# A state-space scan taken two steps at a time, its lagged matrices formed beside the attention, and pieces of the modulation moved

## The reference

```python
def s5_mixer(h, ...):
    u32 = (h @ w_in).reshape(B, L, N_GROUPS, GROUP_CH)     # 64 groups of 16 channels
    dt = jnp.exp(log_dt)[:, None]
    mag = jnp.exp(lr * dt)                                 # decay, per group and state (64 states)
    ab_re, ab_im = mag * jnp.cos(li * dt), mag * jnp.sin(li * dt)
    ...                                                    # bb: b scaled by coef_re, coef_im
    bu_re = jnp.einsum('blgc,gpc->blgp', u32, bb_re)       # bu_im likewise
    x[l] = ab * x[l-1] + bu[l]                             # complex, over the 256 steps
    y = einsum('blgp,gcp->blgc', xr, c_re) - einsum('blgp,gcp->blgc', xi, c_im)
    y = y + d_skip * u32
    g = jax.nn.gelu(y)
    return (g * jax.nn.sigmoid(g @ w_glu + b_glu)) @ w_out

def modulation(cs, w, b):                                  # before each layer of the first block
    shift, scale, gate = jnp.split(cs @ w + b, 3, axis=-1)
x = layer_norm(ALPHA * x + (1.0 + gate) * y, ln_g, ln_b)   # behind each of these layers
```

## Time and profile before

| | us |
|---|---|
| median of 3 runs | 1976.6 (1970.95 to 1981.65) |
| profiled execution, its time | 1973.95 |
| its span in the trace | 1972.0 |
| TensorE busy | 1755.8 (89%) |
| VectorE busy | 1208.2 (61%) |
| ScalarE busy | 853.7 (43%) |
| GpSimd busy | 151.5 (8%) |

### The profile page before, as it was taken

One profiled execution on the slowest core, in us unless ns is written; L12 is line 12 of the kernel. 1 busy time (PEld: TensorE's weight loads), 2 busy tenths in 40 slices (PEclk: granted clock), 3 DMA queues, 4 the chain that ended last, 5 costly groups with the idle time before them and its releaser, 6 DMA issues.

```text
span 1972.0 us, 19778 instructions
## 1 busy us (share of the span) xinstructions
PE 1755.8 (89%) x7767; PEld 1362.8 (69%) x7767; DVE 1208.2 (61%) x1452; ACT 853.7 (43%) x1173; POOL 151.5 (8%) x273
## 2 busy tenths in 40 slices
PE   7767999965998789699999995999999999889998
PEld 3645788752433667587788874788878888667887
DVE  1677677866999566456644575645465444655454
ACT  1542465423222434354434467443354434545343
POOL 1400100014442001000000000000000000000000
PEclk9868999987999889899999997999999999989999
DMA  9538478623000636564456551455545554424552
GB/s 303 215 139 230 171 265 310 229 92 149 1 0 23 224 114 177 156 245 171 139 188 218 187 187 67 171 189 192 182 181 174 188 192 171 171 76 159 192 188 90
DMA packets 164885, 331.18 MB, mean 168 GB/s; under 512 B 38685, under 2 KB 54365, under 8 KB 164154
## 3 DMA queue, kind: packets, MB, share of 16 engines
q1 hardware_dynamic: 143802, 290.53, 42.6%
q0 software_dynamic: 10032, 36.22, 5.6%
q10 hardware_dynamic: 10960, 3.18, 0.7%
HBM read 325.19 MB, written 4.72 MB: 167 GB/s over the span
## 4 chain that ended last, share of the span: by engine, by line
PE 65%; DVE 22%; DMA 4%; ACT 4%; issue 3%; POOL 1%; SPq 0%; DVEq 0%; ACTq 0%; POOLq 0%
PE ps L617 20%; PE ps L619 20%; PE ps L618 20%; DVE wlo L1637 4%; DMA raw<-in_mlp_w 2%; PE ps L702 2%; DVE work L2039 2%; DMA raw<-in_ssm_w_glu 1%; PE ps L1106 1%; ACT whi L1129 1%; DVE work L2045 1%; DVE work L1679 1%; PE ps L709 1%; DMA raw<-in_mla_w_o 1%; DVE work L2044 1%
## 5 line engine op out<-in xcount | busy, mean ns | idle before, releaser
L1637 DVE TENSOR_TENSOR wlo<-raw,whi 128x2048 fp32r<-128x2048 f32 (+2 forms) x247 | 560.7, 2290 | 353.7 <-ACT whi L1129 353.2
L1129 ACT ACTIVATE whi<-raw 128x2048 fp32r<-128x2048 f32 (+2 forms) x247 | 465.3, 1905 | 285.7 <-PE ps L619 172.0
L617 PE MATMUL ps<-whi,xhi 128*128 128x512 f32 (+2 forms) x1244 | 486.7, 391 | 24.0 <-DVE wlo L1637 14.0
L618 PE MATMUL ps<-wlo,xhi 128*128 128x512 f32 (+2 forms) x1244 | 479.1, 385 | 0.0
L619 PE MATMUL ps<-whi,xlo 128*128 128x512 f32 (+2 forms) x1244 | 478.7, 385 | 0.0
L617 PE MATMUL ps<-whi,hhi 128*128 128x512 f32 x736 | 295.8, 402 | 38.6 <-DVE hlo L1642 38.1
L617 PEld LDWEIGHTS ps<-whi,xhi 128*128 128x128 f32 x1244 | 240.9, 194 | 71.7 <-DVE wlo L1637 16.9
L619 PE MATMUL ps<-whi,hlo 128*128 128x512 f32 x736 | 290.0, 394 | 0.0
L618 PE MATMUL ps<-wlo,hhi 128*128 128x512 f32 x736 | 289.9, 394 | 0.0
L619 PEld LDWEIGHTS ps<-whi,xlo 128*128 128x128 f32 x1244 | 240.1, 193 | 45.9
L618 PEld LDWEIGHTS ps<-wlo,xhi 128*128 128x128 f32 x1244 | 241.1, 194 | 43.4
(11 more groups left out here) (318 smaller groups left out, 1798.3 us busy)
## 6 DMA issues: line engine op xcount, KB each, us to landing
raw<-in_mlp_w SPq DMA_DIRECT2D x64, 1024.0 KB, 5.2
raw<-in_ffn_w_gate SPq DMA_DIRECT2D x44, 1024.0 KB, 5.0
...
```

The costliest lines, as they stand in the source:

```text
L617: pe.matmul(o, lh, rh, start=start, stop=False)
L618: pe.matmul(o, lh, rl, start=False, stop=False)
L1129: act.activation(whi[:, c % SPL, 0:n], raw[:, c % RAW, 0:n], ACT.Copy).then_inc(hi_done, 1)
L1637: dve.tensor_tensor(wlo[:, c % RAW, 0:n], raw[:, c % RAW, 0:n], whi[:, c % SPL, 0:n].bitcast(F32), ALU.subtract).then_inc(lo_done, 1)
```

## The change

The recurrence over 256 steps becomes one over 128. The state is kept at odd steps only: x[2k+1] = ab² x[2k-1] + (bu[2k+1] + ab bu[2k]), so the decay is squared (`rho`), the phase counts every second step, and the input has two matrices, B for the odd step and a lagged ab·B for the even one before it. The output at even steps comes from the state of the odd step before (a lagged C·ab) and a same-step matrix G that takes u[2k] directly to y[2k]; at odd steps it is C as before. Channels are kept with even steps in columns 0 to 127 and odd ones in 128 to 255.

As a pair now needs 128 columns, two pairs (a "duo") fill one instruction: 16 turns instead of 32. What has a constant per pair (GpSimd's phase, half of VectorE's, the scans) is issued per pair at half the width. VectorE adds the two products of the rotation back itself (one addition of 512 columns more), and TensorE's output matmuls take the sum.

The new matrices are formed in the MLA phase: `output_lag` (VectorE, six instructions of 1024 columns), a second `input_matrices` (GpSimd), G by 64 small matmuls and its copies (`same_step`), and four more groups of transposes beside the attention. Four blocks of 1 MB are stored instead of two, and GpSimd loads them, two when piece 27 is used up and two when mlp0's last chunk is done. The part of the coefficients that ScalarE and GpSimd compute (exponential, sines) moves ahead of the first projection.

Pieces move: 0 and 1 behind the rotations, 8 and 9 into the attention (fetched by SP behind the column loads), low parts of chunks 6 and 7 into the attention as well, 28 to 31 from around the scan to behind it, and all of 28 to 35 by two or four places. Within mlp0 pieces 17, 22 and 25 come one step earlier, so that none is left in the last step, and `vectors(2)` goes from the glue to the end of mlp0.

```diff
-STAGE = [n % 2 if n < 4 or 28 <= n < 32 else 5 + n % 2 if n < 8 else 2 + (n - 8) % 3 for n in range(4 * len(THIRDS))]
+STAGE = [n % 2 if n < 4 else 5 + n % 2 if n < 12 else 2 + (n - 12) % 3 for n in range(4 * len(THIRDS))]
 ...
# SP
-                if name == "s5" and k == 6:
-                    sp.wait_ge(piece_used, 28)
-                    sp.wait_ge(s5_stored, 32)
-                    sp.dma_start(mod[:, 0:2048], s5_store[0]).then_inc(s5_loaded, 16)
-                    sp.dma_start(mod[:, 2048:4096], s5_store[1]).then_inc(s5_loaded, 16)
...
+            for n in range(8, 12):
+                fetch(sp, n)
...
# TensorE, s5
-                for i in range(-1, PAIRS + 1):
+                for i in range(-1, DUOS + 1):
                     j = i + 1
-                    if j < PAIRS:
-                        m, a = j // 4, 32 * (j % 4)
+                    if j < DUOS:
+                        m = j // 2
                         if j >= 2:
                             pe.wait_ge(bu_rot, j - 1)
                         for r in range(2):
-                            last = pe.matmul(ps[:, j % 2, r * L:(r + 1) * L], s5B[a:a + 32, m, r, :], uT[a:a + 32, m, :], start=True, stop=True)
+                            for odd in range(2):
+                                for pp in range(2):
+                                    a = 64 * (j % 2) + 32 * pp
+                                    last = pe.matmul(ps[:, bu_bank(j) + pp, r * P:(r + 1) * P], s5B[a:a + 32, odd, m, r, :],
+                                                     uT[a:a + 32, m, odd * P:(odd + 1) * P], start=(odd == 0), stop=(odd == 1))
...
-                        for q, (r, x) in enumerate(((0, xa[:, s, 0:L]), (0, xb[:, s, 0:L]), (1, xa[:, s, L:]), (1, xb[:, s, L:]))):
-                            last = pe.matmul(ps[a:a + 32, 2 + m % 2, 0:L], s5C[:, m, r, a:a + 32], x, start=(q == 0), stop=(q == 3))
+                        x = xa[:, e % 2, :]
+                        for r in range(2):
+                            for pp in range(2):
+                                a, n = 64 * (e % 2) + 32 * pp, pp * L + r * P
+                                pe.matmul(ps[a:a + 32, 2 + m % 2, 1:P], s5C[:, 0, m, r, a:a + 32], x[:, n:n + P - 1], start=False, stop=(r == 1))
+                        for r in range(2):
+                            for pp in range(2):
+                                a, n = 64 * (e % 2) + 32 * pp, pp * L + r * P
+                                last = pe.matmul(ps[a:a + 32, 2 + m % 2, P:L], s5C[:, 1, m, r, a:a + 32], x[:, n:n + P],
+                                                 start=(r == 0), stop=(r == 1))
                         last.then_inc(x_used, 1)
-                spread_third(7, (0, 1))
...
                 pe.wait_ge(sig_ok, 2)
-                spread_third(8, (4, 5))
+                spread_third(7, (4, 5))
...
# VectorE
-                    if k < 4:
+                    if k in (1, 3):
                         vectors(k)
-                    else:
+                    elif k == 4:
...
-                pieces = ((12,), (13, 14), (15, 16), (17, 18, 19), (20, 21), (22, 23), (24, 25), (26, 27)) if name == "mlp0" else (
+                pieces = ((12,), (13, 14), (15, 16, 17), (18, 19), (20, 21, 22), (23, 24, 25), (26, 27), ()) if name == "mlp0" else (
...
+                if name == "mlp0":
+                    vectors(2)
...
-                    if n == 0 and i in (0, 1, 5, 6, 7, 8):
-                        piece(i + 2 if i < 2 else i - 1)
+                    if n == 0:
+                        if i in (4, 7):
+                            lo(6 if i == 4 else 7)
+                        elif i < 10:
+                            piece(i + 2 if i < 4 else i + 1 if i < 7 else i)
...
-                        for r in range(2):
-                            steps.did(dve.tensor_tensor_scan(zst[:, r * L:(r + 1) * L], rho[:, e:e + 1].to_broadcast([P, L]),
-                                                             ps[:, 4 + s, r * L:(r + 1) * L], 0.0, ALU.mult, ALU.add))
+                        for pp in range(2):
+                            for r in range(2):
+                                n = pp * L + r * P
+                                steps.did(dve.tensor_tensor_scan(zst[:, n:n + P], rho[:, 2 * e + pp:2 * e + pp + 1].to_broadcast([P, P]),
+                                                                 ps[:, 4 + s, n:n + P], 0.0, ALU.mult, ALU.add))
...
-                        dve.tensor_tensor(xb[:, s, L:], zst[:, 0:L], sin, ALU.mult).then_inc(x_rot, 1)
+                        do(dve.tensor_tensor(b[:, :, 1, :], z[:, :, 0, :], each(sin), ALU.mult))
+                        dve.tensor_tensor(xa[:, s, :], xa[:, s, :], xb[:, s, :], ALU.add).then_inc(x_rot, 1)
...
+            def output_lag():
+
+                dve.wait_ge(s5t_ok, 4)
+                dve.wait_ge(s5p_pool, 3)
...
+                steps.did(dve.tensor_tensor(o_re, re, wide(3), ALU.mult))
+                steps.did(dve.tensor_tensor(o_im, im, wide(3), ALU.mult))
+                do(dve.tensor_tensor(tmp, im, wide(10), ALU.mult))
+                do(dve.tensor_tensor(o_re, o_re, tmp, ALU.add))
+                do(dve.tensor_tensor(tmp, re, wide(10), ALU.mult))
+                dve.tensor_tensor(o_im, o_im, tmp, ALU.subtract).then_inc(s5_lag, 1)
...
# GpSimd, one turn of the phases
-                    r, k = ph[:, s, 0, :], ph[:, s, 1, :]
-                    do(TS(k, iotaf, th[:, i:i + 1], MAGIC, ALU.mult, ALU.add))
-                    do(TS(k, k, -MAGIC, 1.0, ALU.add, ALU.mult))
-                    axpy(iotaf, th_hi[:, i:i + 1], k, r, ALU.subtract)(r).then_inc(turn_r, 1)
+                    for pp in range(2):
+                        q, c = 2 * i + pp, slice(pp * P, (pp + 1) * P)
+                        r, k = ph[:, s, 0, c], ph[:, s, 1, c]
+                        do(TS(k, iotaf, th[:, q:q + 1], MAGIC, ALU.mult, ALU.add))
...
-            for n in range(28, 32):
-                fetch(pool, n)
-            pool.wait_ge(piece_used, 28)
             s5_phases()
-            pool.wait_ge(x_used, PAIRS)
-            for n in range(32, 40):
+            pool.wait_ge(x_used, DUOS)
+            for n in range(28, 40):
                 fetch(pool, n)
```

344 lines of the change are left out of this document (226 added, 118 removed).

## The result

The changed kernel takes 1894.6 us (median of four runs, 1893.4 to 1895.8), against 1973.8 for the kernel before in the same session: a ratio of 0.959, with a 95% interval of 0.956 to 0.963. The profiled execution took 1894.9 us, its span is 1893.1. The forecast was 1884, in a range of 1862 to 1900, and up to 1915 with the rivals (a) to (c).

The account below looks back on a forecast made before the run. It took VectorE to bound the scan. Scan -66.5, entry -23.4, after the scan -18 and MLA +15 sum to -92.9, so 1973.95 became 1881, plus 2.65 for the median 1884; range 1862 to 1900, up to 1915 with rivals.

Parts of the forecast that it names:

- (a): Scan: TensorE becomes the bound as weight loads are not hidden, turn 7.2 us, +16, 1900 us; chance 0.13.
- (c): MLA costs its upper bound (+27) and the entry gains its lower (-16): 1903 us; chance 0.12.
- MLA: MLA phase: output_lag and moved pieces delay the attention and glue by 23 us, a stall gives back 8: +15.
- the entry: Before the first rotation: end of mlp0 -5.2, the rest -18.2 as waits for transfers shrink; together -23.4 us.
- behind the scan: After the last output tile: earlier first columns -12.4, clock staying up -2.3, an earlier piece some -3; together -18 us.
- the end of mlp0: End of mlp0: vectors(2) leaves the glue and pieces come one step earlier, -5.2 us.
- the scan: Scan loop: VectorE's list serves two pairs per turn, 168.2 us to about 102, -66.5.
- T: Scan loop: time of one turn of VectorE's list for two pairs, 6.2 us, bounds 5.7 to 7.0.
- The signs: Right: turns 6.0 to 6.4, VectorE over 95%, first rotation 8 us earlier, columns at clock 1.00; wrong: MLA's glue beyond 195.
- (b): Scan: GpSimd is slowed moderately, turn of 8 us, +29, 1913 us; chance 0.07.
- (d): Scan: the clock stays at its lower level, turn 11 us, +77+6, 1967 us; chance 0.03.
- (e): Scan: GpSimd's fixed cost per instruction makes the turn 14.3 us, +130, 2014 us; chance 0.03.

Follow-up runs that it names:

- experiment 6: The changed kernel with the scan's matmuls of one pair in a row instead of alternating between the duo's two pairs: 1894.2 us.
- experiment 5: The changed kernel without VectorE's addition of 512 columns per turn; TensorE sums the two products in PSUM with 32 output records instead of 16: 1883.6 us.
- Experiment 2: The changed kernel with GpSimd's forming of the input matrices held back until VectorE has finished output_lag: 1883.0 us.
- experiments 1 and 3: Each the changed kernel with one edit: weight chunks 6 to 8 issued before fetches of pieces 2 to 5, 1879.2 us; pieces 0 and 1 at their old places, 1882.8.
- experiment 4: The changed kernel with the two gain rows of s5 loaded three chunks later in SP's queue: 1880.7 us.
- experiment 8: The changed kernel with the end of mlp0 as before (vectors(2) in the glue, old steps of the pieces): 1895.9 us.

## Why the prediction was right, and where it was off

The direction and the main mechanism held: VectorE's list set the old loop and fills 95% of the new one, which costs 6.1 where I had 6.2. MLA and the entry were mis-sized, the clock behind the scan was wrong, and the number came out nearer than these steps deserve.

**The sum.** The forecast gain was 92.9 us; between the spans it is 78.9, 14.0 short. MLA is 8.0 worse than forecast, the entry 6.7, the stretch behind the scan 1.9, the end of mlp0 0.7 and the end of the kernel 1.2; the scan is 4.5 better. MLA at +23.0 and the entry at -16.0 (with mlp0's end) are nearly what rival (c) had, +27 and -16, at a chance of 0.12. That the time still came out 11 us from the forecast is in part luck: the scan's term was better than forecast, and the kernel before ran at 1973.8 beside the changed one, 2.8 below the 1976.6 from which the forecast counts. The range was loose as well: T from 5.7 to 7.0 and MLA from 5 to 27 give 1866 to 1909, not 1862 to 1900.

**The signs.** The turns are 6.1, within 6.0 to 6.4. VectorE is at 94.9%, where I wanted over 95. The first rotation comes 7.0 us later than in the kernel before (475.09 against 468.09), where I had 8 earlier. The first column comes 3.5 behind the last tile, but at a clock of 0.50. And one sign of being wrong came: the glue of MLA stands at 195.62, beyond 195.

**The scan, -71.0 for -66.5,** was right in its parts: a scan of 128 at 0.345 (0.35), the addition at 0.73 (0.69). The phase instruction cut in two costs 0.12 more (I had 0.03), half an output tile 0.20 (0.24). For the collision with GpSimd I had 0.46; it is 0.1 in L2158 and a wait of 0.42 in every second turn, 0.3 a turn. 16 turns of 6.1 are 97.8, the whole stretch: the 2.5 that I had added for filling and emptying aren't there.

**TensorE's turn was sized too high:** 5.8, where the trace has 4.3 (27.80 of 40 us busy, of 6.1). I took 0.11 per record of 128 columns from the attention, where full tiles follow each other; here small tiles seem to run side by side (experiment 6, for the input). So rival (a) had nothing behind it, and experiment 5 could use the slack. Rivals (b), (d) and (e) fell as well: in the loop GpSimd's small instructions took 0.30 to 0.80, which holds VectorE up only in every second turn, and the clock stayed at 1.00 from 480 to the last output.

**MLA, +23 for +15.** The steps that failed are "six instructions of 1024 columns at 1.23 ... 7.4, perhaps 10 beside GpSimd" and "piece 1 is used up some 11.5 later (7.4+5.3, less the idle time)", together with the one that priced the earlier coefficients at nothing. As coefficients and zn are ready early, GpSimd starts its matrices at 68.2 (at 87.4 in the kernel before), right beside output_lag, which takes 12.1. Experiment 2 shows it. The second step doesn't even close: 7.4+5.3-3.9 is 8.8. Piece 1 ends 21.2 later (105.62 against 84.43): 1.5 as VectorE comes to output_lag later, 7.9 by output_lag in place of the idling and the reciprocal, 10.7 by the rotations (6.7 in the kernel before; they now wait 2.73 for TensorE, and three of their instructions take 1.04 to 1.15 instead of 0.28), 1.0 by a slower piece 0. The path from there was as I put it (piece 1, SP's queue, chunk 7, exponential), shown by experiments 1 and 3. The attention's first softmax comes 17.2 later (128.9 against 111.7) and the glue 30.8 later, where I had 23; the stall in front of the next state took back 7.7, as forecast.

**The entry, -11.5 for -18.2.** The step that failed most is "the phase before it", to which my sum leaves 0.8 us: from the end of the low part to the first rotation 7.7 pass (467.42 to 475.09), with 4.65 of waiting for GpSimd's third phase. Also failed: "it lands some 5.5 later, since the 3 to 4 MB beside it are gone". The chunk took 9.4 us, behind 1 MB of rows and beside two more chunks; in the kernel before it took 11.2, so the removed loads were worth 1.8 at most. Against these 10.8 us stands that the chunk left 41.0 behind the state instead of 45.0. What it waited for was the rows' place in the queue (experiment 4, 12.4 us).

**Behind the scan, -16.1 for -18.** Failed: "with a gap of 4 us I expect it to stay up". The gap was 4.1, the clock fell to 0.50 at its start, the first pass 8.7 instead of the forecast 5.75. The other parts came as worked out.

**The end of mlp0,** -4.5 for -5.2, was right (experiment 8).

The Trainium skill ("VectorE: DVE Perf Modes", section on the TRN2 errata) has a fixed cost for each instruction; by an estimate from its formula a split costs 0.16, and T would be 6.5. The trace has 6.1: from start to start two scans of 128 take 0.69 where one of 256 took 0.645, and two phase instructions 0.64 where one took 0.52, so a split cost 0.05 to 0.12. The Trainium skill ("GPSIMD Engine Reference", Key points) has VectorE and GpSimd share SBUF interfaces, with contention when a VectorE instruction has two SBUF inputs. Experiment 2 agrees: such instructions went from 2.2 us to 1.22 and GpSimd's from 2.04 to 1.06 once they no longer ran together. I had used this rule for the scan, where it cost little, and not for output_lag, where it cost most.
